# A hybrid decoder step on one core: twelve operand rows read back in six transfers, and the y blocks split where they lie

## The reference, cut to what matters

```python
h = rmsnorm(x, norm_pre) * (1 + scale) + shift
u = h @ w_in                        # one projection, 13 parts
q_a, k_a, v_a, z_a, q_m, k_m, v_m, o_m, z_m, i_m, f_m, g_a, g_m = split_in(u)
att = rmsnorm(attend(q_a, k_a, v_a)) * (1 - lam_init)
y_a = (att * silu(z_a)) @ w_br_a                        # 1024 -> 2048
hm, C1, n1, m1 = mlstm(q_m, k_m, v_m, i_m, f_m, state)
y_m = (sigmoid(o_m) * rmsnorm(hm) * silu(z_m)) @ w_br_m # 1024 -> 2048
y = (sigmoid(g_a) * y_a + sigmoid(g_m) * y_m) @ w_out   # 2048 -> 2048
out = x + gate * rmsnorm(y, norm_post)
```

## Time and profile before

| | |
|---|---|
| median of 3 runs | 1946.91 us (1945.34 to 1946.96) |
| the profiled execution | 1943.91 us, its span 1942.4 us |
| PE busy | 1886.6 us (97% of the span) |
| PEld / DVE / ACT / POOL busy | 1688.1 / 994.2 / 685.0 / 219.6 us |
| chain that ended last, by engine | PE 88%, DVE 4%, DMA 3% |
| granted PE clock, mean | 0.993 of full speed |
| DMA | 268.97 MB, mean 138 GB/s |

### The profile page before, as it was taken

One profiled execution on the slowest core, in us unless ns is written; L12 is line 12 of the kernel. 1 busy time (PEld: TensorE's weight loads), 2 busy tenths in 40 slices (PEclk: granted clock), 3 DMA queues, 4 the chain that ended last, 5 costly groups with the idle time before them and its releaser, 6 DMA issues.

```text
span 1942.4 us, 33029 instructions
## 1 busy us (share of the span) xinstructions
PE 1886.6 (97%) x13093; PEld 1688.1 (87%) x13093; DVE 994.2 (51%) x2026; ACT 685.0 (35%) x1136; POOL 219.6 (11%) x373
## 2 busy tenths in 40 slices
PE   6999999999999999999999999999999899799997
PEld 4779898988899998888989999999998678678885
DVE  4665234246653334544445777777776443452224
ACT  4212212234544554434323334334344222233332
POOL 2120011100021010113221000000002000100001
PEclk9999999999999999999999999999999999899999
DMA  9996663332134452234433343343446344552223
GB/s 314 322 290 188 203 218 94 81 97 67 52 102 160 148 166 71 76 84 144 124 97 116 100 132 116 121 122 114 132 123 205 111 149 155 176 194 91 82 80 121
DMA packets 190173, 268.97 MB, mean 138 GB/s; under 512 B 16185, under 2 KB 147385, under 8 KB 188873
## 3 DMA queue, kind: packets, MB, share of 16 engines
q1 hardware_dynamic: 167344, 194.03, 32.9%
q0 software_dynamic: 20448, 72.82, 11.2%
q10 hardware_dynamic: 2242, 0.19, 0.1%
HBM read 235.09 MB, written 31.89 MB: 137 GB/s over the span
## 4 chain that ended last, share of the span: by engine, by line
PE 88%; DVE 4%; DMA 3%; SPq 2%; issue 1%; ACT 1%; POOL 1%; DVEq 0%; ACTq 0%
PE gemm L609 63%; PE bank_s L609 11%; PE bank_a L609 6%; PE bank_o L609 5%; SPq L485 2%; DMA ada_in<-in_w_ada 1%; PE bank_s L862 1%; DMA y_back<-y_scratch 1%; DMA y_back<-prod_scratch 1%; DVE g_m L2294 1%; DVE y_tok L2374 1%; PE bank_s L638 0%; PE bank_a L806 0%; DMA w_raw<-in_w_in 0%; PE bank_s L1027 0%
## 5 line engine op out<-in xcount | busy, mean ns | idle before, releaser
L1250 ACT ACTIVATE w_hi<-w_raw 128x512 fp32r<-128x512 f32 x384 | 241.1, 629 | 698.1 <-PE gemm L609 412.5
L1661 DVE TENSOR_TENSOR w_lo<-w_raw,w_hi 128x512 fp32r<-128x512 f32 x384 | 269.5, 703 | 421.9 <-ACT w_hi L1250 421.1
L609 PE MATMUL gemm<-h_hi,w_hi 128*128 128x288 f32 x2048 | 460.8, 306 | 3.8 <-DVE z_act L2246 2.6
L609 PE MATMUL gemm<-h_hi,w_lo 128*128 128x288 f32 x2048 | 438.3, 296 | 0.0
L609 PE MATMUL gemm<-h_lo,w_hi 128*128 128x288 f32 x2048 | 437.2, 295 | 0.0
L609 PEld LDWEIGHTS gemm<-h_hi,w_hi 128*128 128x128 f32 x2048 | 328.1, 189 | 52.2 <-issue 42.8
L609 PEld LDWEIGHTS gemm<-h_hi,w_lo 128*128 128x128 f32 x2048 | 329.0, 188 | 0.0
L609 PEld LDWEIGHTS gemm<-h_lo,w_hi 128*128 128x128 f32 x2048 | 328.7, 188 | 0.0
L1250 ACT ACTIVATE f_hi<-w_all 128x896 fp32r<-128x896 f32 x128 | 120.2, 951 | 176.9 <-PE gemm L609 104.8
L2193 DVE TENSOR_TENSOR f_lo<-w_all,f_hi 128x896 fp32r<-128x896 f32 x128 | 139.4, 1089 | 62.5 <-ACT f_hi L1250 62.2
L609 PE MATMUL gemm<-w_hi,y_all 128*128 128x512 f32 x512 | 158.9, 391 | 0.5 <-DVE g_m L2294 0.5
(11 more groups left out here) (521 smaller groups left out, 3122.7 us busy)
## 6 DMA issues: line engine op xcount, KB each, us to landing
w_raw<-in_w_in SPq DMA_DIRECT2D x256, 256.0 KB, 2.9
ada_in<-in_w_ada SPq DMA_DIRECT2D x72, 512.0 KB, 7.6
w_all<-in_w_in SPq DMA_DIRECT2D x128, 256.0 KB, 3.2
w_raw<-in_w_out SPq DMA_DIRECT2D x64, 256.0 KB, 2.5
gate_scratch<-h_free POOLq DMA_DIRECT2D x32, 288.0 KB, 3.2
ada_gate<-in_w_ada SPq DMA_DIRECT2D x16, 512.0 KB, 5.2
k_page<-in_cache_k POOLq DMA_DIRECT2D x16, 512.0 KB, 5.5
v_page<-in_cache_v POOLq DMA_DIRECT2D x16, 512.0 KB, 4.4
```

The lines of the kernel that those rows point to most:

```text
L609: return nc.tensor.matmul(out, lhsT, rhs, start=start, stop=stop, skip_group_check=True)
L1250: return nc.scalar.activation(out, in_, func, **kw)
L1661: V.tensor_tensor(w_lo[:, slot], w_raw[:, slot], w_hi[:, slot], ALU.subtract).then_inc(lo_ready, 1)
```

## The change

The name of the change speaks of the operand rows; the diff has five parts.

1. Operand rows 4 to 15 are read back in six transfers of two rows (`back_load`), alternately into `y_back` and a new tile `rows_back`. Rows 0 to 3 still come one by one into `att_back`. The ACT and DVE steps for rows 4 to 15 stand 3 granules ahead of PE in place of 6.
2. `y_scratch` is gone, with its twelve stores and twelve loads. The four blocks of a quad are split from `g_a` straight into `y_all`, two in granule 3 and two in granule 4 of the mat that follows (m = 2, 4, 6, 8). The load of the next gates into `g_a` waits for that.
3. `mix` for "ym" does its four gate products first, and then the four additions.
4. The first branch granule waits bank by bank for 4, 6, 7 and 7 products of the last group.
5. The 24 steps of `sums` start four granules earlier and leave out the granule g = 7 of each pass.

```diff
-S_AT = 28 * NG + 6
+S_STEPS = [x for p, steps in ((28, range(2, 7)), (29, range(7)), (30, range(7)), (31, range(5))) for x in (p * NG + g for g in steps)]
...
+        rows_back = sb("rows_back", "ROWS", 0, [P, 2, T])
...
-                            pe.wait_ge(p_free, 7 * GP)
+                            pe.wait_ge(p_free, 7 * (GP - 1) + (4, 6, 7, 7)[b])
...
-                if x - S_F + 6 < 16:
-                    br_hi_of(x - S_F + 6)
+                if 4 <= x - S_F + 3 < 16:
+                    br_hi_of(x - S_F + 3)
...
-                if i == FQ - 1 and kind in ("ya", "ym") and x - S_F - FGRAN * i in range(3, 15):
-                    y_lo(x - S_F - FGRAN * i - 3)
+                if kind in ("ya", "out") and 3 <= kt < 5 and m in (2, 4, 6, 8):
+                    y_lo(2 * m - 4 + 2 * (kt - 3))
+                    y_lo(2 * m - 4 + 2 * (kt - 3) + 1)
...
-                    if kind == "ym":
+                if kind == "ym":
+                    for b in range(4):
                         dve.wait_ge(bank_free[b // 2], V0 + 32 + 2 * m + b % 2 + 1)
-                        V.tensor_tensor(g_a[:, b, 0:TP], g_a[:, b, 0:TP], g, ALU.add).then_inc(mix_ready, 1)
+                        V.tensor_tensor(g_a[:, b, 0:TP], g_a[:, b, 0:TP], g_m[:, b, 0:TP], ALU.add).then_inc(mix_ready, 1)
...
+            def back_load(q):
+                if q < 4:
+                    if q > 1:
+                        pool.wait_ge(br_lo, q - 1)
+                    pool.dma_start(back(q), att_scratch[q]).then_inc(in_att[q % 2], 16)
                 else:
-                    pool.wait_ge(gemm_used, S_F - 1)
-                pool.dma_start(y_back[:, q % 2, :], prod_scratch[q - 8]).then_inc(in_y[q % 2], 16)
+                    if q < 8:
+                        pool.wait_ge(gemm_used, S_F - 1)
+                    else:
+                        pool.wait_ge(br_lo, q - 2)
+                    rows = (att_scratch if q < 8 else prod_scratch)[q % 8:q % 8 + 2].rearrange("q p t -> p q t")
+                    pool.dma_start((rows_back if q % 4 else y_back)[:], rows).then_inc(in_back[q // 2 % 2], 16)
...
+            for q in (2, 3, 4, 6):
+                back_load(q)
             gate_store(GP - 1)
-            pool.wait_ge(br_lo, 8)
+            pool.wait_ge(br_lo, 4)
             pool.wait_ge(gemm_used, S_F)
             ga_load(0)
+            for q in range(8, 16, 2):
+                back_load(q)
             pool.wait_ge(g_out, G_OUT + 32 * GP)
             gm_load(0)
-            for q in range(10, 16):
-                prod_load(q)
             for i in range(FQ - 1):
-                y_store(i)
+                pool.wait_ge(mix_ready, 5 * (i + 1))
                 gm_load(i + 1)
-                pool.wait_ge(y_stored, 64 * (i + 1))
+                pool.wait_ge(y_lo_made, 4 * (i + 1))
                 ga_load(i + 1)
-            for blk in range(12):
-                y_load(blk)
```

More of the change, by code:

```diff
@@ L385, in build, with back @@
         bank_o = ps("bank_o", [P, 512])
+        def back(q):
+            if q < 4:
+                return att_back[:, q % 2, :]
+            return (y_back if q % 4 < 2 else rows_back)[:, q % 2, :]
         def block(cb):
@@ L454, in build @@
         g_out, G_OUT = mst_out, 32 * HM
+        in_back = (in_y[0], in_rows)
         in_att, IN_ATT = (in_k, in_v), 32 * NB
@@ L1530, in _ @@
                 p, g = x // NG, x % NG
-                j, r = divmod(x - S_AT, 3)
-                if 0 <= j < NG and r == 2:
+                j, r = divmod(S_STEPS.index(x), 3) if x in S_STEPS else (NG, 0)
+                if j < NG and r == 2:
                     act.wait_ge(sums_made, S_MADE + j + 1)
@@ L1546, in br_hi_of @@
             def br_hi_of(q):
-                if q < 8:
+                if q < 4:
                     act.wait_ge(in_att[q % 2], IN_ATT + 16 * (q // 2 + 1))
-                    act.wait_ge(gemm_used, S_F - 6 if q < 4 else S_F - 2)
-                    go(bra[q][:, 0:T], att_back[:, q % 2, :]).then_inc(br_hi, 1)
+                    act.wait_ge(gemm_used, S_F - 6)
                 else:
-                    act.wait_ge(in_y[q % 2], 16 * ((q - 8) // 2 + 1))
+                    act.wait_ge(in_back[q // 2 % 2], 16 * (q // 4))
                     act.wait_ge(gemm_used, S_F)
                     act.wait_ge(lo_ready, S_F)
-                    go(brm[q - 8][:, 0:T], y_back[:, q % 2, :]).then_inc(br_hi, 1)
+                go((bra[q] if q < 8 else brm[q - 8])[:, 0:T], back(q)).then_inc(br_hi, 1)
             def split_first(x):
@@ L1585, in y_hi @@
             def y_hi(blk):
[L1586 to L1594, removed]
+                act.wait_ge(mix_ready, 5 * (blk // 4 + 1))
+                if blk == 0:
+                    act.wait_ge(g_out, G_OUT + 32 * GP)
+                go(y_all[:, blk, 0:T], g_a[:, blk % 4, :], scale=0.5).then_inc(y_hi_made, 1)
             def copy_s(m, x):
@@ L1630, in _ @@
                         square_s(i - 1)
-                if i == FQ - 1 and kind in ("ya", "ym") and x - S_F - FGRAN * i in range(3, 15):
-                    y_hi(x - S_F - FGRAN * i - 3)
-                if kind == "out" and i == 0 and 3 <= kt < 7:
-                    y_hi(12 + kt - 3)
+                if kind in ("ya", "out") and 3 <= kt < 5 and m in (2, 4, 6, 8):
+                    y_hi(2 * m - 4 + 2 * (kt - 3))
+                    y_hi(2 * m - 4 + 2 * (kt - 3) + 1)
                 if kind == "out" and kt == 10:
@@ L2239, in _ @@
                     form_lo(1)
-                if 0 <= j < NG:
+                if j < NG:
                     sums(j, r)
@@ L2253, in br_lo_of @@
                 dve.wait_ge(br_hi, q + 1)
[L2254 to L2257, removed]
+                low_part(bra[q] if q < 8 else brm[q - 8], back(q))
             forms_a(1)
@@ L2275, in _ @@
                         forms_b(b)
-                if g >= GG - 6:
+                if GG - 6 <= g < GG - 2:
                     br_lo_of(g - GG + 6)
@@ L2283, in y_lo @@
                 dve.wait_ge(y_hi_made, blk + 1)
-                src = y_back[:, blk % 2, :] if blk < 12 else g_a[:, blk - 12, :]
+                src = g_a[:, blk % 4, :]
                 V.scalar_tensor_tensor(y_all[:, blk, T + NS:2 * T], src[:, 0:TP], 0.5, y_all[:, blk, 0:TP], ALU.mult, ALU.subtract)
@@ L2333, in _ @@
                     split_lo(slot_of(x + LOOKAHEAD), x + LOOKAHEAD)
-                if x - S_F + 6 < 16:
-                    br_lo_of(x - S_F + 6)
+                if 4 <= x - S_F + 3 < 16:
+                    br_lo_of(x - S_F + 3)
                 if kt == 1 and m > NM:
@@ L2343, in _ @@
                         gated_s(i - 1)
-                if i == FQ - 1 and kind in ("ya", "ym") and x - S_F - FGRAN * i in range(3, 15):
-                    y_lo(x - S_F - FGRAN * i - 3)
+                if kind in ("ya", "out") and 3 <= kt < 5 and m in (2, 4, 6, 8):
+                    y_lo(2 * m - 4 + 2 * (kt - 3))
+                    y_lo(2 * m - 4 + 2 * (kt - 3) + 1)
                 if kind == "out" and i == 0:
-                    if 3 <= kt < 7:
-                        y_lo(12 + kt - 3)
                     if kt == 2:
@@ L2566, in state_in @@
                     pool.dma_start(c0[lot][:, b], state_C[0, 4 * lot + b, hd].rearrange("(r p) k -> p r k", p=P)).then_inc(in_c0[lot], 16)
[L2568 to L2578, removed]
             def negM_in(hd):
```

24 lines of the change are left out of this document (6 added, 18 removed).

## The result

The changed kernel takes 1914.22 us (median of 4 runs, 1913.99 to 1914.77) beside 1946.22 of the kernel before (4 runs, 1945.34 to 1946.96): a ratio of 0.9836 [0.9819, 0.9853], 32.0 us less. The profiled execution took 1914.40 us, its span 1912.9, against 1943.91 and 1942.4: 29.5 us less, and -29.9 was the sum. PE is now busy for 1877.1 us (98%), DVE 993.2, ACT 684.8, POOL 204.8; 261.88 MB are moved, 7.1 less.

What follows compares the result with a forecast made beforehand. PE, busy 97% of the span, was taken as the bound, so only its gaps could be won. Terms of -7.0, -14.5, -4.4, -1.4 and -2.6 sum to -29.9 us: 1946.91 - 29.9 = 1917.0, range 1912 to 1926.

Steps and rivals of the forecast that it cites:

- the sum: The five terms added: -7.0 - 14.5 - 4.4 - 1.4 - 2.6 = -29.9 us, 1914.0 for a profiled execution.
- Operand rows (part 1): Quad 0 of the branch stage: with every operand row in time it loses nothing, -7.0 us.
- Rival A: Quad 0: operand rows come late after all, the whole 7.0 us stays, 1924.0; chance 0.09.
- y blocks (part 2): Quad 3: twelve stores and twelve loads go, and with them both stalls, -14.5 us.
- rival D: Quad 3: only the named part works, stalls come from something else such as weight loads and stay, 1931.5; chance 0.04.
- the new wait: Quads 1 to 3: the `g_a` load stands behind the last split; budget 8.7 us, load 8.4, cost 0.
- Rival B: Quads 1 to 3: the `g_a` load lands 2 us over budget each time, +6 us, 1923; chance 0.07.
- E's price: Slower rival, `g_a` load: three stalls each cost length over 8.7 us plus 1.9 for clock; 1950.6 at 18 us; chance 0.02.
- Mix order (part 3): After each "ym" mat, four times: products together keep DVE ahead of PE, saving 1.11 us each, -4.4 us.
- First branch granule (part 4): Start of branch stage: bank 0 needs only the fourth of seven products, PE's 1.43 us wait goes, -1.4 us.
- `sums` (part 5): Three pass ends: PE's waits for `z_act` behind a `sums` step on DVE go, -2.6 us, at worst -1.3.
- Rival C: Small reorderings bring nothing: PE meets another wait, half of parts 3 and 5 lost, 3.5 us, 1920.5; chance 0.08.

Runs made afterwards that it cites:

- the kernel before with two calls swapped: Kernel before, only `g_m` for quad 0 loaded behind operand rows 10 to 15 instead of ahead: 1940.81 us, ratio 0.9969.
- part 2 alone: Kernel before with only the y blocks changed (no `y_scratch`, blocks split from `g_a`): 1930.31 us, ratio 0.9920.
- The two shifted kernels: Changed kernel with the y blocks split one granule later (granules 4 and 5), 1917.54 us, or two later (5 and 6), 1932.59 us.
- the experiment: Changed kernel with product and addition of the "ym" mix alternating per bank as before: 1920.51 us, branch stage +4.4 us.

## Why the prediction was right, point by point

**Operand rows (part 1).** The stall was the operand rows behind `g_m`, and it went as a whole: 7.0 us. That the order was the cause is shown by the kernel before with two calls swapped. Rival A is out: from 1485 to 1530 us ACT waits for no row. Its waits there:

```profile
ACT w_hi L1256 <- PE bank_s L615: 24.6, 13, 2.6
ACT h_free L1256 <- DVE h_free L2224: 2.6, 1, 2.6
ACT s_copy L1256 <- PE bank_s L615: 1.9, 1, 1.9
```

All are for PE and DVE, none for DMA. The transfers of the branch stage:

```profile
g_a<-gate_scratch POOLq DMA_DIRECT2D x4, 1152.0 KB, 6.2
g_m<-gate_scratch POOLq DMA_DIRECT2D x4, 1152.0 KB, 6.0
y_back<-prod_scratch POOLq DMA_DIRECT2D x2, 576.0 KB, 5.6
rows_back<-prod_scratch POOLq DMA_DIRECT2D x2, 576.0 KB, 4.7
```

I had 6.5 us for a pair; medians of 5.6 and 4.7. For a gate load I had taken 8.4 us as the upper end, and quad 0's `g_a` took 10.0: that bound was too low, and it did no harm. Two arguments of this step didn't hold though its size did. I said that the short lead is paid for by two slots of two rows and by `g_m` being moved, as if both were needed. With the new slots and lead, `g_m` ahead loses nothing; with the old ones, `g_m` behind loses nothing in the kernel before and 2.0 us in the new one. And the transfers of two rows are not what helps. Rows 8 and 9, issued at 1492.91, landed 6.9 us later at 1499.82, 0.8 before ACT took the first of them, and with `g_m` first ACT stood 3.0 us for them at no cost to PE:

```profile
1487.59 0.96 POOL L2641 DMA_DIRECT2D g_a<-gate_scratch  x1
1492.91 0.72 POOL L2638 DMA_DIRECT2D y_back<-prod_scratch  x1 [4.36 <-DVE bra L2153]
...
1513.31 0.76 POOL L2644 DMA_DIRECT2D g_m<-gate_scratch  x1
1552.26 0.75 POOL L2641 DMA_DIRECT2D g_a<-gate_scratch  x1 [6.26 <-DVE y_all L2282]
```

**y blocks (part 2).** Both stalls of quad 3 went, 14.5 us as summed, and part 2 alone in the kernel before brings the same 14.45: rival D is out. For the new wait I had counted 0.3 us of slack (a budget of 8.7 for a load of 8.4), and that term was mis-sized. `g_a` went out at 1552.26 in quad 1 and DVE's mix read it at 1559.77:

```profile
1559.77 2.48 DVE L2290 SCALAR_TENSOR_TENSOR g_a<-g_a,gemm 128x512 f32<-128x512 f32 x4
```

In quads 1 to 3 the load took 5.7 to 6.2 us where I took the old 8.4. The two shifted kernels measure the slack: one granule (3.2 us) later PE stands 0.67 us on average, two (6.4) later 3.73, so it is 2.5 to 2.7 us. Rival B is out for the changed kernel, but its mechanism is real: only the place of the split keeps it away. The form of E's price held too: 1.9 us for the clock at each stall, and 2.0 measured in the mean of three (1.4 to 2.6), (17.1 - 11.2) / 3 with 17.1 the loss in the three granules (8.76 + 8.18 + 9.76 - 3 x 3.20).

**Mix order (part 3).** 1.1 us four times, 4.4 in the experiment. The waits for `g_m` came to only 2.2 us before: idle time shows half of what the order cost. **First branch granule (part 4).** The branch stage's first matmul starts 0.34 us after the start of the last form matmul, which itself takes 0.29; before it was 1.72. The prediction asked for within 0.3. **`sums` (part 5).** 2.8 us for 2.6 (2.1 to 3.3 over all the profiles), no pass end waits, and undoing it brings three waits back. Rival C, half of parts 3 and 5 lost, is out.

**The sum.** In the profiled executions -29.5 stands against -29.9. The median gained 32.0. My step from one to the other, adding the 3.0 us by which the median of before lay above its profile, was the weak one: the profiled run of before was faster than any of its timed runs, while that of after is one with its median (1914.40 and 1914.22). Over the profiles of all these kernels the stretch from the start to ACT's first `z_act<-gemm`, where their code is the same, differed by 4 us (763.3 to 767.6). So 1917.0 was 2.8 us high, and the offset accounts for it: 1914.0 for a profiled execution stands against 1914.4. That the timed runs of before spent their extra time in that same stretch is likely and not shown, since none of them has a profile.

## What to carry to other kernels

Ask of a small load that others wait for what stands ahead of it in its queue: one large load there cost 7.0 us, and swapping two calls was the cure (5.3 of 7.4 once PE came sooner), while joining the small loads was worth nothing. A round trip through HBM that only serves to reorder work should be tried against splitting the data where it lies; then shift that step by one and by two granules, for the slack is worth knowing, and the fall behind it is steep (2.8 us, then 17.6). Measure small effects by the distance between the same instruction in successive granules.

## What the runs showed of the hardware

Gaps of PE of 3.56 to 5.53 us in the branch stage were each followed by a granted clock of 0.50 to 0.67 over the next 4.5 us, at or between the levels of 1.2 and 2.4 GHz. Ahead of each gap, but for the second one of quad 3, it had been 1.00. After gaps of 1.78 us and less it stayed at 1.00. The granule at such a gap cost 1.4 to 3.0 us over the idle time. What lies between 1.78 and 3.56 I did not try.

In the changed kernel a transfer of 576 KB took 4.2 to 6.9 us, and 10.9 with `g_m` first, behind two gate loads of 1152 KB. Gate loads of quads 1 to 3 took 8.1 to 8.9 us in the kernel before, with the stores of y and each other under way, and 5.7 to 6.2 in the changed one, where neither was; which of the two slows them is not shown. In quad 0 the changed kernel's took 10.0 and 9.2 us, with operand rows behind or ahead of them.
